# New places in SBUF for the tiles of a two-model transformer kernel: weights at one offset modulo 512 bytes, activation operands 256 bytes away

## The reference, cut to what matters

```
h = rmsnorm(x, mix_norm); z = h @ w_in
merged = g_a * (o_a @ w_branch_a) + g_b * (o_b @ w_branch_b) + g_c * (o_c @ w_branch_c)
x = x + merged @ w_out
x = x + (silu(h2 @ w_ffn_gate) * (h2 @ w_ffn_up)) @ w_ffn_down
```

## The kernel before

| stretch (us from the start) | line | activation high, low | weights high | weight operand minus activation operand, in the three steps |
|---|---|---|---|---|
| 81 to 153 | 480 | 224, 224 | 288 | 64, -96, 64 |
| 247 to 281 | 480 | 96, 288 | 288 | 192, -160, 192 |
| 318 to 431 | 480 | 96, 128 | 288 | 192, 0, 192 |
| 1106 to 1120 | 480 | 384, 128 | 224 | -160, 0, -160 |
| 1325 to 1359 | 480 | 96, 128 or 96 | 256 | 160, 0 or 32, 160 |
| 2092 to 2137 | 480 | 96, 128 | 352 | 256, 0, 256 |
| 19 to 75 | 488 | 224, 224 | 288 | 64, 64, -96 |
| 431 to 486 | 488 | 96, 96 | 288 | 192, 192, 32 |
| 1135 to 1147 | 488 | 384, 128 | 224 | 96, -160, -256 |
| 2167 to 2178 | 488 | 96, 128 | 352 | 224, 256, 32 |

## Time and profile before

### The profile page before, as it was taken

One profiled execution on the slowest core, in us unless ns is written; L12 is line 12 of the kernel. 1 busy time (PEld: TensorE's weight loads), 2 busy tenths in 40 slices (PEclk: granted clock), 3 DMA queues, 4 the chain that ended last, 5 costly groups with the idle time before them and its releaser, 6 DMA issues. The chain is left out here.

```text
span 3030.8 us, 35565 instructions
## 1 busy us (share of the span) xinstructions
PE 2586.0 (85%) x13090; PEld 1885.0 (62%) x13090; DVE 2113.4 (70%) x4116; ACT 1087.8 (36%) x1979; POOL 607.0 (20%) x573
## 2 busy tenths in 40 slices
PE   8999999999999899899887666678999887666766
PEld 7968997896899797797543222226888653222222
DVE  6467665657765565555898888866674699888876
ACT  4365444436444465444221111113644222112111
POOL 0000000000000000001445444440000254444442
PEclk9999999999999999999998888889999998988888
DMA  6423554441455433254999999997434899999997
GB/s 255 172 100 126 183 183 152 180 174 70 157 181 187 152 140 113 96 181 160 418 427 421 427 426 426 427 427 295 165 112 146 343 418 423 426 426 427 426 426 306
DMA packets 112493, 810.80 MB, mean 268 GB/s; under 512 B 12736, under 2 KB 12736, under 8 KB 14272
## 3 DMA queue, kind: packets, MB, share of 16 engines
q0 software_dynamic: 73728, 536.90, 42.2%
q1 hardware_dynamic: 38592, 271.63, 24.5%
HBM read 807.44 MB, written 1.05 MB: 267 GB/s over the span
## 5 line engine op out<-in xcount | busy, mean ns | idle before, releaser
L3511 PE MATMUL ps<-arena 128*128 128x512 f32 x912 | 522.2, 724 | 239.1 <-ACT arena L3407 239.0
L167 DVE TENSOR_TENSOR ring_low<-ring,parts 128x2048 fp32r<-128x2048 f32 x214 | 488.0, 2291 | 310.6 <-ACT parts L161 306.8
L480 PE MATMUL ps<-parts,parts 128*128 128x256 f32 x2528 | 569.7, 283 | 2.5 <-PEq L393 1.7
L3511 PEld LDWEIGHTS ps<-arena 128*128 128x128 f32 x912 | 201.9, 231 | 547.0 <-ACT arena L3407 321.0
L480 PE MATMUL ps<-parts,ring_low 128*128 128x256 f32 x1824 | 511.9, 281 | 0.0
L161 ACT ACTIVATE parts<-ring 128x2048 fp32r<-128x2048 f32 x214 | 406.8, 1913 | 274.6 <-PE ps L488 105.7
L488 PE MATMUL ps<-parts,parts 128*128 128x512 f32 x1344 | 439.0, 396 | 5.8 <-DVE ring_low L167 3.8
L480 PEld LDWEIGHTS ps<-parts,parts 128*128 128x128 f32 x2528 | 428.1, 189 | 3.7 <-issue 2.1
L3234 POOL DMA_INDIRECT arena<-in_experts,stage_index x276 | 323.0, 1170 | 531.7 <-PE ps L3511 224.2
L3511 PE MATMUL ps<-ring,arena 128*128 128x512 f32 x616 | 316.0, 650 | 106.5 <-ACT arena L3407 106.2
L3282 DVE CUSTOM_DVE_ANT_0 arena<-arena 128x1024 f32<-128x1024 f32 x276 | 333.6, 1227 | 96.9 <-DMA arena<-in_experts,stage_index 94.0
(11 more groups left out here) (504 smaller groups left out, 2968.0 us busy)
## 6 DMA issues: line engine op xcount, KB each, us to landing
ring<-in_stream SPq DMA_DIRECT2D x249, 1024.0 KB, 4.8
arena<-in_experts,stage_index POOLq DMA_INDIRECT x276, 22.9
ring<-in_experts,stage_index POOLq DMA_INDIRECT x236, 24.6
gain_row<-in_gain_rows SPq DMA_DIRECT2D x4, 512.0 KB, 5.7
arena<-in_mem SPq DMA_DIRECT2D x2, 1024.0 KB, 4.8
arena<-in_stream SPq DMA_DIRECT2D x2, 1024.0 KB, 8.2
par<-in_params SPq DMA_DIRECT2D x4, 386.0 KB, 4.4
x<-in_x SPq DMA_DIRECT2D x1, 1024.0 KB, 4.8
```

Source lines behind the costliest of these rows:

```text
L167: dve.tensor_tensor(k.ring_low[v % SLOTS], whole, self.high_of(v).bitcast(F32), ALU.subtract).then_inc(self.ph.sem("chunk_split"), 1)
L480: last = pe.matmul(self.ps[:, 2 * pair + f // 2, (f % 2) * T:(f % 2 + 1) * T], w[:, f * P:(f + 1) * P], x[:, k, :], start=(k == 0 and i == ...
L3511: last = pe.matmul(k.ps[:, bank + n, :], diag[:, s % ROWS, :], rows[row_of[s]][:, D + n * BLK:D + (n + 1) * BLK], start=(s % SLOTS_PER_TOK ...
```

## The change

The program's tiles are placed anew, and nothing that is computed changes. `rope` moves ahead of `x` and `hT`, so that these begin at 384 modulo 512; a filler tile before the arena makes it begin there too. `weights(a)` rounds a place in the arena up to one that is 128 modulo 512 (as the ring is), and `operand(a)` to one that is 384. All high tiles of weights (`Split.high`, `branch_high`) go through the first, the bases of the activation tiles through the second. A few small tiles move for it: `kcmpT` and `vcmp` of the compressed attention go from the arena into `hT`, the expert layer's `iota`, `dots`, `acts` and `weights` into a new small tile `peer_small`. Each of the three steps above then has its operands 256 bytes apart. The arena's row buffers for the gathers come to 128 modulo 256. One chunk of weights of the cross-attention keeps a place of its own (line 2804, high part at 384).

```diff
-ARENA = 28600
+ARENA = 28608
+LINE = 128
+WEIGHTS_AT = 64
...
+def operand(a):
+    return -(-a // LINE) * LINE
...
+def weights(a):
+    return operand(a - WEIGHTS_AT) + WEIGHTS_AT
...
-        self.high, self.end = k.at_parts(start, self.HIGH_SLOTS, CHUNK)
+        self.high, self.end = k.at_parts(weights(start), self.HIGH_SLOTS, CHUNK)
...
         self.ring, ring_offset = sb_placed("ring", [P, SLOTS, CHUNK])
+        self.rope = sb("rope", [P, 2, MT, 48])
         self.x = sb("x", [P, MT, D])
...
+        self.par = sb("par", [P, PAR_W])
+        self.peer_small = sb("peer_small", [P, 3 * ROWS + PE_TOP])
+        to_line = (hT_offset - nc.sbuf_base) // 4 % LINE
+        self.to_line = sb("to_line", [P, to_line])
         self.arena, self.arena_offset = sb_placed("arena", [P, ARENA])
+        assert (self.arena_offset - hT_offset) % (4 * LINE) == 0
+        assert (self.arena_offset + 4 * WEIGHTS_AT - ring_offset) % (4 * LINE) == 0
...
-        self.branch_high, _ = k.at_parts(a, CHUNK)
+        self.branch_high, _ = k.at_parts(weights(a), CHUNK)
...
+        a = operand(a)
         self.x_high, b = k.at_parts(a, KT, T)
...
-        self.kcmpT, a = k.at(a, N_CMP)
-        self.vcmp, a = k.at(a, 2, HD)
...
+        self.kcmpT, b = k.in_hT(b, N_CMP)
+        self.vcmp, b = k.in_hT(b, 2, HD)
...
+        a = operand(a)
         h_high, _ = k.at_parts(a, KT, T)
...
-MIX_HIGH = 15440
+MIX_HIGH = 15488
...
-        self.iota, a = k.at(a, PE_TOP)
+        self.iota = k.peer_small[:, 3 * ROWS:3 * ROWS + PE_TOP]
...
-        self.dots, a = k.at(a, ROWS)
-        self.acts, a = k.at(a, ROWS)
-        self.weights, a = k.at(a, ROWS)
+        self.dots, self.acts, self.weights = (k.peer_small[:, i * ROWS:(i + 1) * ROWS] for i in range(3))
...
         self.rows, a = k.at(a, 4, 2 * D)
+        a = operand(a)
         self.late_start = a
```

More of the change, by code:

```diff
@@ L310, in __init__ @@
         self.ring, ring_offset = sb_placed("ring", [P, SLOTS, CHUNK])
+        self.rope = sb("rope", [P, 2, MT, 48])
         self.x = sb("x", [P, MT, D])
         self.hT, hT_offset = sb_placed("hT", [P, KT, T])
-        self.par = sb("par", [P, PAR_W])
         self.gain_row = sb("gain_row", [P, D])
@@ L318, in __init__ @@
         self.band = sb("band", [P, 2 * P])
-        self.cmp_mask = sb("cmp_mask", [P, MT, N_CMP])
-        self.row_valid = sb("row_valid", [P, MT])
         self.upper = sb("upper", [P, P])
@@ L323, in __init__ @@
         self.chunk_upper = sb("chunk_upper", [P, P])
-        self.rope = sb("rope", [P, 2, MT, 48])
         self.stat = sb("stat", [P, 8, 64])
+        self.stage_index = sb("stage_index", [P, MT * SLOTS_PER_TOKEN], U32)
+        self.cmp_mask = sb("cmp_mask", [P, MT, N_CMP])
+        self.row_valid = sb("row_valid", [P, MT])
         self.unit = sb("unit", [P, 2])
-        self.stage_index = sb("stage_index", [P, MT * SLOTS_PER_TOKEN], U32)
+        self.par = sb("par", [P, PAR_W])
+        self.peer_small = sb("peer_small", [P, 3 * ROWS + PE_TOP])
+        to_line = (hT_offset - nc.sbuf_base) // 4 % LINE
+        self.to_line = sb("to_line", [P, to_line])
         self.arena, self.arena_offset = sb_placed("arena", [P, ARENA])
+        assert (self.arena_offset - hT_offset) % (4 * LINE) == 0
+        assert (self.arena_offset + 4 * WEIGHTS_AT - ring_offset) % (4 * LINE) == 0
         self.ring_low = [self.parts(f"ring_low{s}", ring_offset + s * CHUNK * 4, CHUNK)[:] for s in range(SLOTS)]
```

## The result

The changed kernel takes 3051.44 us in the median of four runs (3050.88 to 3054.47), the kernel before 3031.49 beside it (3030.45 to 3032.72). The ratio is 1.0068, 95% interval [1.0054, 1.0083]: slower by 0.7%, where 3007 us and a gain of 0.8% were forecast, and outside the range of 2978 to 3027. The profiled execution has a span of 3049.1 us against 3030.8: 18.3 us to account for.

The account below looks back on a forecast made before the run. TensorE's fp32r matmuls were taken to bound most stretches, gathers the two expert stretches. Line 480's 23.5 us plus line 488's 3.2, times 0.92, gave 24.6 us: 3031.7 to 3007.1 us, range 2978 to 3027.

Parts of the forecast that it names:

- Line 480, the term of 23.5 us: 256-column fp32r matmuls at line 480: 118.3 to 114.0 ns a step, 4.3 ns x 5472 = 23.5 us gained.
- d = 114.9 at 256: Line 480: step time at distance 256, 114.9 ns, from the 2092 us series and equations giving each distance its own time.
- Line 488, 3.2 us: 512-column fp32r matmuls at line 488: 231.4 to 230 ns, 3.2 us gained; ends 18.4 us gain, 19.4 us loss.
- The gathers, taken as nothing: Arena's row buffers going from 0 to 128 modulo 256: no effect taken; bounds from the rows nothing to 16 us.
- A rival that held this mechanism: Expert stretches: gathers slower by their places, 24.6 us gained and 16 to 21 lost, 3023 to 3028 us; chance 0.03.
- The moved small tiles, nothing: `kcmpT`, `vcmp` and the expert layer's tiles: same writers, readers and waits at new addresses, cost nothing.
- 92% on the path: Lines 480 and 488: share of the matmul gain reaching the total time, (23.5 + 3.2) x 0.92 = 24.6 us.
- No effect: Matmul paces at lines 480 and 488 differ for another reason, new places change nothing: 3031 us; chance 0.11.
- Load-bound pace: Disturbance gone altogether: line 480 at 110.3 ns, line 488 at 223.4, some 57 us gained, 2975 us; chance 0.20.
- Slower, by line 488: Line 488's step at 256 costs 239.8 ns, 19.4 us lost; with line 480 at 117 ns, 3043 us; chance 0.06.
- A small gain: Line 480 at 116 ns and the gain swallowed in part: 3020 to 3027 us; chance 0.03.
- even but at 117 to 118: Sign that the forecast is wrong: matmul series at line 480 at one pace, but 117 to 118 ns, not near 114.

Follow-up runs that it names:

- the last variant: The changed kernel with the arena 32 bytes lower, high tiles of weights at 96 and of activations at 352 modulo 512: 3044.12 us in one run.
- The first and third experiment: Changed kernel with arena's row buffers back at 256 modulo 512: 3035.67 us; changed kernel moved up 128 bytes, ring at 256, arena's rows at 0: 3034.73 us.

## Why the prediction was wrong

**Line 480, the term of 23.5 us: wrong in sign.** The step that failed is "d = 114.9 at 256". It came out of three equations in which each distance has a time of its own. Measured, every series with all steps at 256 goes at 120.0 ns, outside the ends given ("from above, the step can't be shown to be over what it is now"). (119.94 - 118.05) x 5472 = +10.3 us, where -23.5 were forecast. Two things were wrong in it. A step's time is not its distance's alone: where the high and the low operand stand 32 bytes apart, steps at 0 modulo 256 go at 113 to 119, and where all stand at one place at 120. And a single series was taken for its placement, while the last variant shows one placement at 116.3 and at 118.0 ns. What "the step at 0" gave in the equations (117.5) and what "the step at 256" gave (114.9) should also have been one number, since the experiment with distance 0 repeats that with 256. The six paces compared were also not quite alike: those of 96 and 120 steps held 0.7 to 0.9 ns a step of the series' start, the 960-series 0.1.

**Line 488, 3.2 us: right in sign, too small.** (231.6 - 227.23) x 2304 = 10.1 us gained, inside the ends of 18.4 and -19.4. The reading that a step at 256 might be slow (239.8 ns) was wrong; at 0 or 256 this shape is at its best of all distances tried.

Together they cancel: +10.3 - 10.1 = +0.2 us. The first stretch, up to the first gather, is 0.2 us longer; the middle stretch of 284 us is 3.8 us longer. There too the lines nearly cancel, by an estimate from their paces: the 115.8 ns series lost 384 x 4.4 ns = 1.7 us, and line 505 gained about as much. The granted clock is 0.98 there against 0.99, which would be 2.9 us of 284, an estimate from two digits. The first and third experiment, at distance 256 with the gathers' rate restored, measured 0.14% and 0.13% over the kernel before, some 4 us where the sum gives 0.2. Their mean granted clock over 11 runs each was 0.939, against 0.943 and 0.942 in 15 runs of the kernel before. That fits, and no run shows that the clock is the cause, nor why it was lower.

**The gathers, taken as nothing: wrong, and the bigger part.** Measured +14.3 us of the 18.3, inside the prediction's own bound of 16. The step that failed is the ground for dismissing it, that "the queue moved 427 GB/s with half of its gathers at such places already". That showed what a mixture does. The experiments show that the mixture is free either way round and the full set is not: 427 to 421 GB/s. A rival that held this mechanism stood at 0.03 and its 3023 to 3028 us were made with TensorE's gain of 24.6 us, which did not come.
The Trainium skill's rule (DMA: Bandwidth & Descriptors, How a descriptor splits into AXI transactions), a transaction more for an 8 KB row off a 256-byte boundary, had the right direction for the full set. The size of 21 us was the bound of 8 beats; a row that begins 128 bytes above a boundary ends with 128 bytes over, 4 beats on 256 as that section's table counts, so the estimate should have been 1.6% of 276 x 2.46 us = 11 us; measured were 14.3. The section also words the rule for what a transaction reads, while here it is the place written to that changed. The traces do not follow its beats: rows at 64, 96, 128 and 192 modulo 256 all went at 421 to 422 GB/s, and the rule does not say that unaligned gathers cost next to nothing beside aligned ones, which the traces show.

**The moved small tiles, nothing: right.** The split stands at 2291 ns, and the products wait 2.2 and 5.8 us in all, as before (2.5 and 5.8).

**92% on the path.** Not tested by the changed kernel, as with a sum of 0.2 us there was nothing to lose. The version at distance 64 bears on it: 22.8 us by its paces, 23.0 us of span, so about all of the gain in these matmuls arrived.

**The rivals.** *No effect* (0.11) came nearest for TensorE, for the wrong reason: the new places do change both paces, in opposite directions.
The Trainium skill's rule of two independent ports (TensorE: Matmul & The Clock Gate, Part 2: What happens when you issue a matmul) gives 0 us too, but the distances tried give 113 to 120 ns and 227 to 234 ns for the same instructions at the full clock. The traces so disagree with one pace for all places; by what mechanism the places act they do not show. *Load-bound pace* (0.20) found no support: no series went under 113 ns. *Slower, by line 488* had the wrong line: that one gained. *A small gain* did not come.

**What would show it.** Of the signs listed, "even but at 117 to 118" was the nearest, at 120; "DMA in the expert windows under 420 GB/s" was drawn too low to see a loss of 14 us: 536.9 MB of gathers take 1257 us at 427 GB/s and 1274 us at 421.5. "ScalarE's wait shorter" went the other way with TensorE's pace, 104.5 to 108.1 us.

**What stays open.** Which of its paces a series takes. Behind the first steps it keeps it to its end in almost all cases, and series with equal addresses differ; how each series begins was not varied. Nor is it shown by what mechanism the gathers of a mixed set escape the cost.

## What to carry to other kernels

A rate measured on a mixture is no bound for the pure case: ask of each half that moves whether the other half had been covering it, and put one kind of buffer back by itself, which costs one run. Read several series of the same placement, each without its first steps, before a difference of 2 ns is given to the placement. Decide places for each consumer apart: here matmul operands and weights 64 bytes apart and the arena's rows for the gathers on a multiple of 256 gain 0.6%, where one rule for all tiles lost 0.7%.

## What the runs showed of the hardware that was not expected

- The pace of fp32r matmuls in a series (128x128 loaded, 256 or 512 columns moved) depends on where the tiles of activations and of weights stand relative to each other, modulo 256 bytes: 113.5 to 120.1 ns and 227.2 to 233.7 ns at the full clock. What is best for one shape is worst for the other (120.0 and 227.2 at distance 0).
- At distances 64 and 192, and with steps 32 bytes apart, a series has two paces (behind its first steps 113.3 or 117.8 ns; 115.6 or 117.8) with equal addresses, in one execution as between two variants; at distance 96 there are three (117.3, 118.7, 120.0).
- Gathers of 8 KB per partition run at 426 to 427 GB/s if either the ring's or the arena's row buffers stand on a multiple of 256 bytes, and at 421 to 422 GB/s if none do. With the rows aligned and the ring at 32 modulo 256 it was 425 to 426. The ring's packets of 8192 bytes take 309.3 to 310.0 ns in the first case (311.7 with the ring at 32) and 314.0 in the second.
